# Weight blocks of a decoder layer's first half laid out on the host, one transfer a block

## The reference

```
xn = rmsnorm(h); proj = xn @ w_in            # 1024 -> 2632: q|k|v|index q|index k|index w|pool|memory q
attention over the 64 keys a token that the indexer picks; causal pooling; cross-attention into 256 memory tokens
gates = sigmoid(xn @ w_gate + b_gate)        # 1024 -> 3 x 1024
h = h + (sum over 3 branches: gate * (y_branch @ w_proj_branch)) @ w_out
h = h + moe(rmsnorm(h))                      # top 4 of 32 experts, w_up 1024 -> 2048, w_down 1024 -> 1024 each
out = rmsnorm(h)
```

## Time and profile before

| | us |
|---|---|
| median of 3 runs | 1244.95 |
| lowest and highest | 1244.4, 1247.13 |
| the profiled execution | 1245.37 |
| its span in the trace | 1243.1 |

### The profile page before, as it was taken

One profiled execution on the slowest core, in us unless ns is written; L12 is line 12 of the kernel. 1 busy time (PEld: TensorE's weight loads), 2 busy tenths in 40 slices (PEclk: granted clock), 3 DMA queues, 4 the chain that ended last, 5 costly groups with the idle time before them and its releaser, 6 DMA issues.

```text
span 1243.1 us, 14759 instructions
## 1 busy us (share of the span) xinstructions
PE 1138.4 (92%) x5609; PEld 509.2 (41%) x5609; DVE 389.5 (31%) x797; ACT 226.5 (18%) x415; POOL 128.3 (10%) x59
## 2 busy tenths in 40 slices
PE   5899878998999999999999898999999799999996
PEld 5778778954333333333332223322232233322222
DVE  3593886623222222222222222222222122222222
ACT  5353335312111111111111111111111111111112
POOL 4662445700000000000000000000000000000000
PEclk9999999998999999999999998999999999999999
DMA  9554323488999999999999999999999999999994
GB/s 353 178 176 150 119 70 135 174 337 343 417 417 417 417 417 417 416 417 417 417 418 418 417 417 415 417 418 417 418 418 418 416 416 418 418 417 417 417 417 174
DMA packets 93026, 444.53 MB, mean 358 GB/s; under 512 B 8750, under 2 KB 11352, under 8 KB 60088
## 3 DMA queue, kind: packets, MB, share of 16 engines
q1 hardware_dynamic: 89488, 439.67, 87.4%
q10 hardware_dynamic: 3464, 3.84, 1.0%
HBM read 442.43 MB, written 1.05 MB: 357 GB/s over the span
## 4 chain that ended last, share of the span: by engine, by line
PE 41%; SPq 33%; DMA 11%; DVE 7%; issue 4%; ACT 3%; ACTq 0%; POOL 0%; DVEq 0%
SPq L451 33%; PE psum L1474 14%; PE psum L1176 10%; PE psum L1510 8%; PE psum L1363 2%; DMA gate_area<-in_w_up 2%; DMA qk_area<-in_w_up 2%; DMA ring<-in_w_up 2%; DMA mem_s<-in_w_up 2%; DMA xT_area<-in_w_up 2%; PE psum L1430 2%; DVE gate_area L1109 1%; DVE gate_area L1107 1%; DVE gate_area L1113 1%; PE psum L1497 1%
## 5 line engine op out<-in xcount | busy, mean ns | idle before, releaser
L1474 PE MATMUL psum<-ring,gate_area 128*64 128x512 f32 x1312 | 311.9, 608 | 32.2 <-DMA ring<-in_w_up 21.2
L1079 DVE TENSOR_TENSOR h_s<-psum,h_s 128x512 f32<-128x512 f32 x132 | 81.9, 683 | 437.4 <-PE psum L1430 437.4
L1474 PEld LDWEIGHTS psum<-ring,gate_area 128*64 128x64 f32 x1312 | 89.5, 139 | 240.7 <-issue 167.9
L1510 PE MATMUL psum<-ring,gate_area 128*64 128x512 f32 x640 | 145.8, 595 | 5.3 <-ACT gate_area L758 5.3
L515 POOL TENSOR_TENSOR unit_lo<-ring,unit_hi 128x1024 fp32r<-128x1024 f32 (+1 forms) x54 | 127.9, 2379 | 118.2 <-ACT unit_hi L548 118.2
L752 ACT ACTIVATE gate_area<-gate_area 128x512 f32<-128x512 f32 x32 | 20.1, 629 | 552.4 <-DVE gate_area L1105 552.4
L1105 DVE TENSOR_SCALAR gate_area<-psum 128x512 f32<-128x512 f32 x32 | 22.1, 692 | 286.0 <-PE psum L1483 286.0
L1510 PEld LDWEIGHTS psum<-ring,gate_area 128*64 128x64 f32 x640 | 44.4, 136 | 86.2 <-issue 76.0
L1430 PE MATMUL psum<-pT_s,gate_area 64*128 64x512 f32 x264 | 65.6, 615 | 0.7 <-ACT pT_s L762 0.7
L548 ACT ACTIVATE unit_hi<-ring 128x1024 fp32r<-128x1024 f32 (+1 forms) x54 | 55.5, 1033 | 49.3 <-PE psum L1176 49.1
L1411 PE MATMUL psum<-xn_area,gate_area 128*64 128x512 f32 x264 | 64.1, 606 | 0.4 <-DVE gate_area L1051 0.4
(11 more groups left out here) (262 smaller groups left out, 1261.8 us busy)
## 6 DMA issues: line engine op xcount, KB each, us to landing
ring<-in_w_up SPq DMA_DIRECT2D x164, 1024.0 KB, 20.7
ring<-in_w_down SPq DMA_DIRECT2D x80, 1024.0 KB, 24.8
gate_area<-in_w_up SPq DMA_DIRECT2D x16, 1024.0 KB, 20.6
xT_area<-in_w_up SPq DMA_DIRECT2D x16, 1024.0 KB, 23.0
ring<-in_w_gate SPq DMA_DIRECT2D x6, 2048.0 KB, 8.9
qk_area<-in_w_up SPq DMA_DIRECT2D x12, 1024.0 KB, 20.8
mem_s<-in_w_up SPq DMA_DIRECT2D x12, 1024.0 KB, 21.2
yl_area<-in_w_up SPq DMA_DIRECT2D x12, 1024.0 KB, 21.6
```

Of the source, the lines that this page charges most:

```text
L1079: nc.vector.tensor_tensor(h_s[:, b, cols], psum[:, BACK_BANKS[j], :], h_s[:, b, cols], ALU.add).then_inc(added, 1)
L1474: ins = nc.tensor.matmul(psum[lo:lo + SLOTS, c, :], lhsT, w[:, at:at + 512], start=(k == 0), stop=False)
L1510: ins = nc.tensor.matmul(psum[c * SLOTS:(c + 1) * SLOTS, DOWN_BANK, :], lhsT, w[:, at:at + 512], start=(f == 0), stop=(f == KC - 1))
```

## The change

The host builds one array `front` of 128 rows (one for each partition) and 66,112 columns, in which all of a block that goes to one partition lies side by side: 16 KB for a 2,048 KB block, 10.25 KB for A, 8 KB for QM. The distance from one partition's row to the next is 264,448 bytes. SP moves each block with one transfer of 128 such pieces. PPM was two transfers and is one; the wait for it (`both_arrived`) counts accordingly. The order of the blocks, the slots, the waits in front of each block and all other engines' instructions are as they were. The seven weight arrays that the blocks came from are no longer arguments of the kernel.

```diff
+FRONT_W = {"A": KC * A_W, "QM": KC * 256}
+FRONT_W = {name: FRONT_W.get(name, RS) for name in FRONT}
+FRONT_AT = {name: sum(FRONT_W[m] for m in FRONT[:n]) for n, name in enumerate(FRONT)}
...
             block_arrived(eng, "PA")
-            n = FRONT.index("PPM")
-            eng.wait_ge(got_block[n % RING_SLOTS], 16 * (n // RING_SLOTS + 2))
+            block_arrived(eng, "PPM")
...
-                for ap, at in src[name]:
-                    k, cols = ap.shape[1], ap.shape[2]
-                    s = (n % RING_SLOTS) * RS + at
-                    dst = ring[:, s:s + k * cols].rearrange("p (k n) -> p k n", n=cols)
-
-                    sp.dma_start(dst, ap).then_inc(got_block[n % RING_SLOTS], 16)
+                s, width = (n % RING_SLOTS) * RS, FRONT_W[name]
+                sp.dma_start(ring[:, s:s + width], front[:, FRONT_AT[name]:FRONT_AT[name] + width])\
+                  .then_inc(got_block[n % RING_SLOTS], 16)
...
+def front_blocks(data):
...
+    def rows(w):
+        return w.reshape(-1, P, w.shape[-1]).transpose(1, 0, 2)
...
+    return np.concatenate([src[name].reshape(P, -1) for name in FRONT], axis=1)
```

More of the change, by code:

```diff
@@ L162, in unit_read, with hybrid_layer_kernel @@
     return "bank_filled", FILLED["br", j, 2] if name == "P" else FILLED["gate", 4 * int(name[1]) + j]
-def hybrid_layer_kernel(nc, x, mem, w_in, w_gate, w_proj_attn, w_proj_pool, w_proj_mem, gains, pool_w_group,
-                        w_mem_kv, w_out, norm_ffn_g, w_router, b_router, w_up, b_up, w_down, b_down,
+def hybrid_layer_kernel(nc, x, mem, front, gains, pool_w_group, norm_ffn_g, w_router, b_router, w_up, b_up, w_down, b_down,
                         norm_final_g, ident_c, iota_c, before_c, causal_c, rope_c, pool_c, expert_c, out):
@@ L417, in _ @@
                 sp.dma_start(h_s[:, b, :], x[0, b * P:(b + 1) * P, :]).then_inc(got_x[b], 16)
[L418 to L426, removed]
             for n, name in enumerate(FRONT):
@@ L1541, in shape_constants @@
             "pool": pool, "expert": expert}
-_INS = ["x", "mem", "w_in", "w_gate", "w_proj_attn", "w_proj_pool", "w_proj_mem", "gains", "pool_w_group", "w_mem_kv",
-        "w_out", "norm_ffn_g", "w_router", "b_router", "w_up", "b_up", "w_down", "b_down", "norm_final_g",
+def front_blocks(data):
+    import numpy as np
+    def rows(w):
+        return w.reshape(-1, P, w.shape[-1]).transpose(1, 0, 2)
+    win, wgt, wo = rows(data["w_in"][0]), rows(data["w_gate"][0]), rows(data["w_out"][0])
+    src = {"A": win[:, :, C_IK:C_QM], "IQ": win[:, :, C_IQ:C_IK], "Q": win[:, :, C_Q:C_K], "K": win[:, :, C_K:C_V],
+           "V": win[:, :, C_V:C_IQ], "QM": win[:, :, C_QM:IN_W], "KV": rows(data["w_mem_kv"][0]),
+           "PA": rows(data["w_proj_attn"][0]),
+           "PPM": np.concatenate([rows(data["w_proj_pool"][0]), rows(data["w_proj_mem"][0])], axis=1),
+           "O0": wo[:, :, 0:512], "O1": wo[:, :, 512:1024]}
+    for g in range(6):
+        src[f"G{g}"] = wgt[:, :, 512 * g:512 * (g + 1)]
+    return np.concatenate([src[name].reshape(P, -1) for name in FRONT], axis=1)
+_INS = ["x", "mem", "front", "gains", "pool_w_group", "norm_ffn_g", "w_router", "b_router", "w_up", "b_up", "w_down", "b_down", "norm_final_g",
         "c_ident", "c_iota", "c_before", "c_causal", "c_rope", "c_pool", "c_expert"]
@@ L1559 @@
     data["norm_final_g"] = data["norm_final_g"].reshape(1, D)
+    data["front"] = front_blocks(data)
     for k, v in shape_constants().items():
```

## The result

The kernel with the new layout takes **1256.09 us** (median of 4 runs, 1254.66 to 1257.21) where the one before takes 1244.89: a ratio of 1.0086, 95% interval 1.0070 to 1.0102. It is 11.2 us slower; 1244.5 was forecast, with a range to 1248.5. The profiled execution took 1257.21, its span is 1255.0, 11.9 us more than before.

The account below looks back on a forecast made before the run. The front's chain of computing was taken to bound the kernel by setting when the expert stream begins. Terms 0 - 0 - 0.4 + 0 moved it up 0.4 us, giving 1244.5 us; range 1241.5 to 1248.5.

Parts of the forecast that it names:

- The bound of the kernel: Whole kernel: the end is when the expert stream can begin, set by the front's computing, plus its bytes at 417 GB/s.
- Blocks land earlier and nobody waits: Front's blocks: each lands 0 to 0.5 us sooner, but every block has cover already, so worth 0 on the path.
- the 18 to 20.5 that I gave: Sign in the changed profile: block IQ would land at 18 to 20.5 us; it landed at 21.38 before.
- no copy was released by a block: Sign at ACT's copy of IQ's first unit: the prediction is wrong if a transfer releases `unit_hi` of IQ.
- SP's queue no longer fills: SP's issues of Q and K, 4.50 and 8.84 us, fall under 1 us; worth 0, since V waits for POOL anyway.
- The 0.4 us for ACT's issues: ACT's nine issues ahead of `xT_hi`: shorter once SP's queue isn't full; 0.4 us gained, within 0 to 1.4.
- Large pieces beside small ones: ACT's small transfers beside SP's 16 KB pieces: constants land at about 38 to 41 us, needed at 62.3; cost 0.
- ACT's queue fills: Rival at ACT's issues before `xT_hi`: stuck 5.6 us per transfer of 128 pieces too many; 1250 for one, 1261 for three; 5%.
- The prediction's figures for SP: SP's queue: some 2,535 pieces outstanding at the end of K's issue, 2,725 at the end of Q's.
- The new layout doesn't read slowly: Rival on block reads: pieces 264,448 bytes apart might halve the pace, delaying IQ and Q, giving 1250.6 us; chance 4%.
- The expert stream's pace: Rival in the expert loop: arrays may lie elsewhere in DRAM; 0.3% of pace is 2.9 us; 12% faster side, 2% slower.

## Why the prediction was wrong

**The bound of the kernel: right.** The end is set by when the expert stream can begin, and that by the front's computing. The expert loop's slices are unchanged.

**Blocks land earlier and nobody waits: right.** IQ landed at 16.6 us, outside the 18 to 20.5 that I gave and on the good side; no copy was released by a block. The two runs with late `br_s` show the layout's own worth as nothing that their times can tell (1244.48 and 1244.68 us).

**SP's queue no longer fills: right** (Q's and K's issues 0.47 and 0.43 us). **The 0.4 us for ACT's issues: not there.** The first seven span 7.09 to 10.78 us, 3.69, where they spanned 7.21 to 10.97, 3.76. Their length hardly depends on SP's full queue.

**Large pieces beside small ones: the step that failed.** Its term in the sum was 0, and the hold measured 10.1 us at the start of `xT_hi` (11.4 us of issue in place of 1.1). Its facts held: one for one, some 23 pieces a microsecond forecast (29 in 12 to 18 us), the constants late but not waited for. The cost was put at 0 because I asked only who waits for the *landing*. The one who waits was the engine that *issues*. I did have that as the rival "ACT's queue fills", with its place (ahead of `xT_hi`), its price (5.6 us a transfer of 128 pieces; measured 6.9 and 4.4, and 128 packets drained between the ends of the two) and its time: 1250 for one transfer, 1261 for three, so 1256 for the two that were held. That the sum of the two holds fits so well, 11.35 us for 11.2, is in part luck: 222 packets drained in the first and 128 in the second. What was wrong is its chance of 5%. It rested on a single argument, that SP's queue holds over 2,500 pieces, and no row showed ACT's queue beside large pieces. The trace of before does show 1,472 of ACT's packets outstanding with nothing held, so a fixed limit of 1,200 was not to be had from it either; what it could not show is that ACT is held sooner beside larger pieces. The rival named about 1,200 pieces outstanding as the count that decides, with some 330 drained by 12.5 us. Only 90 packets had drained by then, so ACT's queue was fuller than the rival itself supposed. The prediction's figures for SP, 2,535 and 2,725, are somewhat high: they took the drained pieces from landing times, while the trace counts 4,720 - 2,396 = 2,324 packets outstanding at the end of K's issue and 3,680 - 1,115 = 2,565 at the end of Q's. In my judgement the rival deserved a far greater chance, and the range should have reached to 1256: a limit known only for another queue, and only beside small pieces, says little here.

**The other rivals.** The new layout doesn't read slowly: 2.63 MB in 6 us of 12 to 18 us, 438 GB/s, more than the 376 to 390 of before. The rule of the Trainium skill on row pitches that the prediction cited ("DMA: Bandwidth & Descriptors", section on latency and other measured facts) spoke against this rival, and the trace agrees at this pitch. The expert stream's pace moved neither way.

## What to carry to other kernels

Merging DRAM rows into larger pieces made SP's queue faster here and ACT's slower, because the two queues were served one piece of each in turn. Ask then not only who waits for the small transfers to land but who issues them: the copies that stood behind ACT's held issues could not start. So keep the transfers of an engine that computes off its critical path (here worth 1.5 to 2 us, with the old layout too), or keep the neighbour's pieces small while it issues (at 4 KB no loss could be told from noise). A layout change is worth nothing where each block has cover.

## What the runs showed of the hardware that I had not expected

- The two queues are unequal. At the ends of its held issues SP had 2,565 and 2,324 packets outstanding (2 KB pieces, the kernel before), ACT 1,270 and 1,286 (the changed kernel).
- When ACT's queue lets a transfer in depends on the other queue: beside 16 KB pieces at 1,110 to 1,147 earlier packets left, beside 8 KB at 1,196 and 1,210, and beside 2 KB it was not held with 1,472 outstanding in all. One transfer went in at 1,279 beside 16 KB pieces without a hold, so this is no fixed number of places.
- The granted clock of the same work differs from one execution to the next. For the first matmuls after 14 to 15 us without work it reads 0.50 in the changed kernel and 1.00 where only the first four blocks are new.
- The granted clock doesn't tell the whole of PE's pace. In 16.2 to 20.5 us of the kernel before it reads 1.00, and its 328-column matmuls are 0.27 us apart, as they are at 0.50 in the changed kernel; from 20.7 us on they are 0.15 apart.
